# Two transformer blocks in one kernel: the six norm boundaries taken by token tile instead of for both tiles at once

## The chip, the cores and the metric

The kernel runs on one core of one Trainium2 chip. A core has TensorE (PE; PEld is its weight load), VectorE (DVE), ScalarE (ACT), GpSimd (POOL) and SyncE (SP), each with its own instruction stream, which wait for each other through semaphores. The metric is the device time of one execution in microseconds (us), lower is better.

## The reference

One batch of 256 tokens with 1024 features goes through two blocks of one layer each, in float32. Cut to what matters here:

```
def first_block(x, p, positions, ...):
    h = x
    h = h + 0.5 * swiglu(rms_norm(h, ffn1_norm), ffn1_w_in, ffn1_w_out)      # norm n1; hidden width 2816
    u = rms_norm(h, mix_norm)                                                # norm n2
    proj = u @ w_in                     # latents (672 columns), stick-breaking q, k, v, gates
    ... two attentions, merged = g_mla * (o_mla @ w_branch_mla) + g_sb * (o_sb @ w_branch_sb)
    h = h + merged @ w_out
    h = h + 0.5 * swiglu(rms_norm(h, ffn2_norm), ffn2_w_in, ffn2_w_out)      # norm n3
    ple_gate = sigmoid(rms_norm(h, ple_norm) @ w_ple_gate)                   # norm n4
    return h + ple_gate * (p @ w_ple_proj)

def second_block(x, ...):
    proj = rmsnorm(x, attn_norm) @ w_in                                      # norm n5
    ... sparse attention, state-space branch, gates -> merged
    x = x + merged @ w_out
    return x + hier_moe(rmsnorm(x, ffn_norm), router weights, 32 experts)    # norm n6

def rms_norm(x, g):
    r = rsqrt(mean(x * x, axis=-1) + 1e-6)
    return (x * r) * g
def swiglu(u, w_in, w_out):
    a, b = split(u @ w_in, 2)
    return (silu(a) * b) @ w_out
```

## The kernel before, in words

**Data.** X holds the 256 tokens as two tiles of 128 partitions (tokens) by 1024 columns. A norm's output is kept turned: Uh and Ul are 8 chunks of 128 features (partitions) by 256 tokens. Every float32 operand of a matmul is split into a high part and a rest (h and l), and a product is three matmuls (`mm3`): high by high, high by rest, rest by high.

**Weights.** They come in slabs of 1 MB (8 chunks of 128 rows by 256 columns), which SP loads into three slots (NSLOT = 3), each in two halves. ACT copies a half to the high part (L464) once the slab three before it has been used up, and DVE subtracts to get the rest (L470). A semaphore `lo_done` counts halves, `slab_used` counts slabs that PE has finished. `hi_upto(name)` and `lo_upto(name)` issue the splits up to two slabs behind the one named.

**A norm boundary.** X is updated in four parts of 256 columns, both tiles in each. Then ACT takes the sum of squares of each tile (L581), POOL the inverse root (L590, L594), DVE scales a tile into xn (L607), PE transposes the tile's 8 chunks (L621) into banks 4 to 7, both tiles of a chunk side by side, ACT copies with the gain to Uh (L585; for n1 L1340), 8 instructions of 256 columns, and DVE makes Ul (L611), 8 of 256 columns. PE then starts the first matmuls of what follows chunk by chunk as Ul grows. ACT begins with the copies when both tiles are transposed.

**What follows the norms.** After n1 and n3 come the feed-forward loops (`pe_ffn`), 11 rounds of two slabs up (96 matmuls that move 256 token columns) and one slab down (24 that move 512). Four matmuls with zeros (L633) clear the four banks that gather the result. After n2 come the latent slabs `lat0` to `lat2`, after n4 `pproj` (which needs no norm) and four slabs `pgate`, after n5 the slabs `q0`, `q1` and so on, after n6 the router (36 columns), between rows of matmuls with zeros that only keep PE at work (L2509). The slabs `wout` (before n3), `pgate` (before n5) and `wo` (before n6) are matmuls with 128 tokens as weights that move 256 weight columns, tile 0 and then tile 1 in each slab.

**Order.** Every engine's order is the order in which the code is written; nothing reorders it. On ACT, behind the splits of the first three slabs, stand the issue of eleven DMAs of constants (L1343 to L1348, among them the token positions) and two sines of the rotation angles (L1351, L1352), which wait for DVE (L1719) and so for the positions; behind them the first Silu (L675).

Of the kernel before, what the change touches and what calls it, by code (L numbers as in the profile page):

```python
# [15 lines left out]
P = 128  # L16
# [80 lines left out]
def two_blocks(nc, a, out):  # L97
    with ExitStack() as ctx:
        def sb(name, shape, dt=F32, scope=ctx):
# [14 lines left out]
                   (("ss", NT), ("tr", KD // 2), ("hi", KD), ("r", NT), ("xn", NT), ("lo", KD))],  # L114
# [350 lines left out]

        def split_lo(i, q=None):
# [110 lines left out]
        def act_norm(nm, ready, gain):  # L577

            for t in range(NT):
                act.wait_ge(*reach(ready[0], ready[1 + t]))  # L580
                act.activation(xn[:, t], X[:, t], ACT.Square, accum_out=stat("norm", 4)[:, t:t + 1]).then_inc(S(nm + "_ss"), 1)  # L581
            for j in range(KD // 2):
                act.wait_ge(*reach(nm + "_tr", j + 1))
                for c in range(2):
                    act.activation(Uh[:, 2 * j + c], bank[4 + j][:, c * T:(c + 1) * T], ACT.Copy,  # L585
                                   scale=gcol(gain, 2 * j + c)).then_inc(S(nm + "_hi"), 1)
# [17 lines left out]
        def dve_norm(nm, gain):  # L604
            for t in range(NT):
                dve.wait_ge(*reach(nm + "_r", t + 1))
                dve.tensor_scalar(xn[:, t], X[:, t], stat("norm", 4)[:, 2 + t:3 + t], None, ALU.mult).then_inc(S(nm + "_xn"), 1)  # L607
            for j in range(KD // 2):
                dve.wait_ge(*reach(nm + "_hi", 2 * j + 2))
                for c in range(2):  # L610
                    dve.scalar_tensor_tensor(Ul[:, 2 * j + c], bank[4 + j][:, c * T:(c + 1) * T], gcol(gain, 2 * j + c),  # L611
                                             Uh[:, 2 * j + c].bitcast(F32), ALU.mult, ALU.subtract).then_inc(S(nm + "_lo"), 1)

        def pe_norm(nm):
            for t in range(NT):
                pe.wait_ge(*reach(nm + "_xn", t + 1))
                for j in range(KD // 2):
                    if t == 0:
                        claim(4 + j, nm + "_lo", 2 * j + 2)
                    for c in range(2):  # L620
                        last = pe.transpose(bank[4 + j][:, c * T + t * P:c * T + (t + 1) * P],  # L621
                                            xn[:, t, (2 * j + c) * P:(2 * j + c + 1) * P], ident)
                    if t == NT - 1:
                        last.then_inc(S(nm + "_tr"), 1)
            fresh.append((nm + "_lo", 1, Uh))

        def pe_ffn(nm, n):
            b = slab_of[nm]  # L630
# [29 lines left out]
            up(None, b)  # L660
# [564 lines left out]

        gate2_bank = (7, 4, 7, 0, None, None, 6, 7)
# [99 lines left out]
        def _(_e):  # L1326
# [29 lines left out]
            act_norm("n2", ("ffn1_x", 2, 4), "mix_norm")  # L1356
# [1238 lines left out]
```

## Time and profile before

| | us |
|---|---|
| median of 3 runs | 1460.13 (1456.04 to 1461.11) |
| the profiled execution | 1461.1 |
| its span, from the first to the last instruction | 1459.2 |
| PE busy in it | 1359.7 (93%) |
| PE's weight load busy | 1233.4 (85%) |
| DVE busy | 942.3 (65%) |
| ACT busy | 755.8 (52%) |
| mean granted TensorE clock | 0.967 of full |

PE's stream is almost full, so time is lost where PE waits, where its clock is at the lower of its two levels (1.0 of full is 2.4 GHz, 0.5 is 1.2 GHz), and where its instructions get little done each. Durations of matmuls are longer than the distance from one to the next, since they overlap. What a matmul costs in a dense stretch is the length of the stretch divided by the number of matmuls in it; some records are missing and some at the edges are counted, so such a quotient is good to some per cent.

### The profile page before, as it was taken

What the parts mean: (1) busy time and instruction counts of PE and PEld (TensorE: products, weight loads), DVE (VectorE), ACT (ScalarE), POOL (GpSimd) and SP (SyncE); (2) the same over time, 40 slices, a digit from 0 to 9 for tenths busy, and PEclk for the clock granted to TensorE, in tenths of its full rate; (3) what the DMA queues carried; (4) which work ended last, traced back from release to release, by engine and by line L of the source; (5) the groups of instructions that cost most, each with busy time, mean ns of one, the idle gap of its engine ahead of it and who ended that gap; (6) DMA issues with size and microseconds to landing.
All of it is one profiled execution on the core that took longest, in us unless ns stands there. A gap on an engine that the chain in (4) does not pass through costs nothing.

```text
span 1459.2 us, 22962 instructions
## 1 busy us (share of the span) xinstructions
PE 1359.7 (93%) x9038; PEld 1233.4 (85%) x9038; DVE 942.3 (65%) x1363; ACT 755.8 (52%) x1108; POOL 171.6 (12%) x131
## 2 busy tenths in 40 slices
PE   6999999979898999998978997998999999999997
PEld 5999989978698999988977776898999778787776
DVE  4655564473575555565488664575575789999996
ACT  4343344545644343455354556433563577777774
POOL 0211120111001122110020000340000000202020
PEclk9999999989999999999989999999999999999999
DMA  7665645542154655544524222233556299999991
GB/s 243 212 190 178 196 136 162 160 136 96 45 168 141 188 188 184 188 146 143 159 87 144 88 87 87 87 87 93 176 166 205 87 354 366 365 368 351 364 338 60
DMA packets 222164, 263.43 MB, mean 181 GB/s; under 512 B 14017, under 2 KB 204798, under 8 KB 221950
## 3 DMA queue, kind: packets, MB, share of 16 engines
q1 hardware_dynamic: 219520, 260.39, 55.6%
q10 hardware_dynamic: 2558, 1.86, 0.4%
q8 instruction: 58, 0.95, 0.3%
q14 instruction: 28, 0.23, 0.0%
HBM read 261.17 MB, written 1.05 MB: 180 GB/s over the span
## 4 chain that ended last, share of the span: by engine, by line
PE 75%; DVE 14%; ACT 6%; issue 3%; DMA 1%; POOL 1%; ACTq 0%; DVEq 0%; POOLq 0%
PE bank L526 23%; PE bank L528 22%; PE bank L527 22%; DVE sb_wlo L483 3%; DVE sb_wlo L470 3%; ACT sb_whi L464 1%; DVE sb_XC L1870 1%; PE bank L2474 1%; PE bank L621 1%; DMA sb_pos<-in_positions 1%; ACT sb_aw L1542 1%; PE bank L2537 1%; DVE sb_st L1120 1%; DVE sb_aw L1902 1%; ACT sb_sgh L1115 0%
## 5 line engine op out<-in xcount | busy, mean ns | idle before, releaser
L470 DVE TENSOR_TENSOR sb_wlo<-sb_raw,sb_whi 128x1024 fp32r<-128x1024 f32 (+4 forms) x306 | 389.3, 1316 | 239.1 <-ACT sb_whi L464 238.9
L464 ACT ACTIVATE sb_whi<-sb_raw 128x1024 fp32r<-128x1024 f32 (+4 forms) x306 | 301.4, 1037 | 238.6 <-PE bank L528 238.4
L526 PE MATMUL bank<-sb_Uh,sb_whi 128*128 128x256 f32 x1216 | 352.2, 290 | 5.9 <-DVE sb_wlo L470 4.8
L527 PE MATMUL bank<-sb_Ul,sb_whi 128*128 128x256 f32 x1216 | 349.2, 287 | 0.0
L528 PE MATMUL bank<-sb_Uh,sb_wlo 128*128 128x256 f32 x1216 | 348.9, 287 | 0.0
L526 PEld LDWEIGHTS bank<-sb_Uh,sb_whi 128*128 128x128 f32 x1216 | 239.0, 197 | 11.2 <-issue 8.9
L527 PEld LDWEIGHTS bank<-sb_Ul,sb_whi 128*128 128x128 f32 x1216 | 239.1, 197 | 0.8
L528 PEld LDWEIGHTS bank<-sb_Uh,sb_wlo 128*128 128x128 f32 x1216 | 238.6, 196 | 0.0
L526 PE MATMUL bank<-sb_whi,sb_Uh 128*128 128x256 f32 (+3 forms) x560 | 159.8, 285 | 1.1 <-DVE sb_Ul L611 0.7
L527 PE MATMUL bank<-sb_wlo,sb_Uh 128*128 128x256 f32 (+3 forms) x560 | 159.2, 284 | 0.0
L528 PE MATMUL bank<-sb_whi,sb_Ul 128*128 128x256 f32 (+3 forms) x560 | 159.1, 284 | 0.0
L526 PE MATMUL bank<-sb_whi,sb_hh 128*128 128x512 f32 x288 | 113.3, 393 | 3.2 <-DVE sb_hl L907 3.2
L528 PE MATMUL bank<-sb_whi,sb_hl 128*128 128x512 f32 x288 | 112.5, 391 | 0.0
L527 PE MATMUL bank<-sb_wlo,sb_hh 128*128 128x512 f32 x288 | 112.5, 391 | 0.0
L526 PEld LDWEIGHTS bank<-sb_whi,sb_Uh 128*128 128x128 f32 x560 | 108.8, 194 | 2.5 <-issue 1.9
L527 PEld LDWEIGHTS bank<-sb_wlo,sb_Uh 128*128 128x128 f32 x560 | 108.9, 194 | 0.0
L528 PEld LDWEIGHTS bank<-sb_whi,sb_Ul 128*128 128x128 f32 x560 | 108.8, 194 | 0.0
L526 PE MATMUL bank<-sb_whi,sb_SUh 128*128 128x512 f32 x256 | 104.2, 407 | 0.7 <-DVE sb_wlo L483 0.7
L528 PE MATMUL bank<-sb_whi,sb_SUl 128*128 128x512 f32 x256 | 102.0, 398 | 0.0
L527 PE MATMUL bank<-sb_wlo,sb_SUh 128*128 128x512 f32 x256 | 101.7, 397 | 0.0
L483 DVE TENSOR_TENSOR sb_wlo<-sb_raw,sb_whi 128x1024 fp32r<-128x1024 f32 x76 | 90.9, 1220 | 9.3 <-ACT sb_whi L478 9.2
L478 ACT ACTIVATE sb_whi<-sb_raw 128x1024 fp32r<-128x1024 f32 x76 | 78.7, 1057 | 29.5 <-PE bank L528 29.5
(408 smaller groups left out, 2251.8 us busy)
## 6 DMA issues: line engine op xcount, KB each, us to landing
sb_raw<-in_w_in SPq DMA_DIRECT2D x104, 512.0 KB, 4.4
sb_raw<-in_ffn_w_in SPq DMA_DIRECT2D x88, 512.0 KB, 4.6
sb_raw<-in_ffn_w_out SPq DMA_DIRECT2D x44, 512.0 KB, 3.7
sb_raw<-in_w_down SPq DMA_DIRECT2D x26, 512.0 KB, 7.0
sb_raw<-in_w_gate SPq DMA_DIRECT2D x25, 512.0 KB, 6.9
sb_raw<-in_w_up SPq DMA_DIRECT2D x25, 512.0 KB, 6.9
sb_raw<-in_w_out SPq DMA_DIRECT2D x16, 512.0 KB, 4.6
sb_raw<-in_w_ssd_branch SPq DMA_DIRECT2D x16, 512.0 KB, 4.6
```

The source lines that it names most:

```text
L464: nc.scalar.activation(whi[:, i % NSLOT, c], raw[:, i % NSLOT, c], ACT.Copy).then_inc(S("hi_done"), 1)
L470: nc.vector.tensor_tensor(wlo[:, i % NSLOT, c], raw[:, i % NSLOT, c], whi[:, i % NSLOT, c].bitcast(F32), ALU.subtract).then_inc(S("lo_done ...
L478: act.activation(whi[:, i % NSLOT, c], buffers[buffer_of[i]][:, c], ACT.Copy).then_inc(S("hi_done"), 1)
L483: dve.tensor_tensor(wlo[:, i % NSLOT, c], buffers[buffer_of[i]][:, c], whi[:, i % NSLOT, c].bitcast(F32), ALU.subtract).then_inc(S("lo_don ...
L526: pe.matmul(o, lh, rh, start=start, stop=False, skip_group_check=True)
L527: pe.matmul(o, lh, rl, start=False, stop=False, skip_group_check=True)
L528: return pe.matmul(o, ll, rh, start=False, stop=stop, skip_group_check=True)
L621: last = pe.transpose(bank[4 + j][:, c * T + t * P:c * T + (t + 1) * P], xn[:, t, (2 * j + c) * P:(2 * j + c + 1) * P], ident)
L1120: dve.tensor_reduce(stat(nm, 2 * H)[:, t * H:(t + 1) * H], scr[:, 0:H * d].rearrange("p (h d) -> p h d", d=d), AX, ALU.add).then_inc(S(nm ...
L1542: act.activation(aw[:, i % 3, lo:hi], aw[:, i % 3, lo:hi], ACT.Exp, bias=nmx[:, 2 * i + t:2 * i + t + 1], scale=HD ** -0.5, accum_out=sm[: ...
L1870: dve.scalar_tensor_tensor(XC[:, ch, s_:T], sgh[:, j % 2, c * T:(c + 1) * T - s_], gcol("conv_w_2", (TAPS - 1 - s_) * NX + ch), XC[:, ch, ...
L1902: dve.tensor_tensor_reduce(out=aw[:, i % 3, lo:hi], in0=bank[i % 3][:, lo:hi], in1=SELB[:, lo:hi], scale=1.0, scalar=-3e38, op0=ALU.add, o ...
```

## The change

All six norms are taken by token tile. The transposes of a tile go into two banks of their own (even chunks in one, odd chunks in the other; `turn_banks`), ACT and DVE then work on 128 columns at a time, 16 instructions each instead of 8, and ACT's copy of chunk c waits for DVE's work on chunk c - 2, which lies in the same bank.

The output projections before n3, n5 and n6 are taken in pairs of slabs. Each bank then holds one tile by 512 columns. In the second pair both slabs are first used for tile 0 and then for tile 1, so that tile 0 of X is complete a quarter of the projection before its end; its transposes stand inside the last quarter. X is updated by (tile, 512 columns).

What follows a norm starts with tile 0 alone. In the feed-forward parts the first two slabs are taken as tile 0, tile 0, tile 1, tile 1, so each of their matmuls moves 128 columns and there are twice as many; the four zero matmuls stand behind them. `lat0`, `q0` with `q1`, and the router are taken by tile with the same matmuls as before. `pproj` is taken by tile and in halves of 512 columns, one tile ahead of the transposes of n4's tile 0 and one ahead of those of tile 1.

For n1, ACT and DVE split the first two slabs between tile 0 and tile 1 of the norm.

```
-        def pe_norm(nm):
-            for t in range(NT):
-                pe.wait_ge(*reach(nm + "_xn", t + 1))
-                for j in range(KD // 2):
...
-                    for c in range(2):
-                        last = pe.transpose(bank[4 + j][:, c * T + t * P:c * T + (t + 1) * P],
-                                            xn[:, t, (2 * j + c) * P:(2 * j + c + 1) * P], ident)
+        def act_turned(nm, t, gain, chunks=range(KD)):
+            for c in chunks:
+                act.wait_ge(*reach(nm + "_tr", 2 * t + c % 2 + 1))
+                if c >= 2:
+                    act.wait_ge(*reach(nm + "_lo", KD * t + c - 1))
+                act.activation(Uh[:, c, tile_cols(t)], turn_out(nm, t, c), ACT.Copy, scale=gcol(gain, c)).then_inc(S(nm + "_hi"), 1)
+        def dve_turned(nm, t, gain, chunks=range(KD)):
+            for c in chunks:
+                dve.wait_ge(*reach(nm + "_hi", KD * t + c + 1))
+                dve.scalar_tensor_tensor(Ul[:, c, tile_cols(t)], turn_out(nm, t, c), gcol(gain, c),
+                                         Uh[:, c, tile_cols(t)].bitcast(F32), ALU.mult, ALU.subtract).then_inc(S(nm + "_lo"), 1)
+        def pe_turn(nm, t):
+            pe.wait_ge(*reach(nm + "_xn", t + 1))
+            for odd in range(2):
+                claim(turn_banks[nm][2 * t + odd], nm + "_lo", KD * t + KD - 1 + odd)
+                for c in range(odd, KD, 2):
+                    last = pe.transpose(turn_out(nm, t, c), xn[:, t, c * P:(c + 1) * P], ident)
+                last.then_inc(S(nm + "_tr"), 1)
+        def feature_tile(i, b, t, xh, xl, nm=None, at_chunk=None):
+            wh, wl = wslab(i, KD, 256)
+            for k in range(KD):
+                if at_chunk is not None and k == at_chunk[0]:
+                    at_chunk[1]()
+                if k in (0, KD // 2):
+                    pe.wait_ge(*reach("lo_done", 2 * i + (2 if k else 1)))
+                if nm is not None:
+                    pe.wait_ge(*reach(nm + "_lo", KD * t + k + 1))
+                for n in range(2):
+                    f = slice(n * P, (n + 1) * P)
+                    last = mm3(bank[b][:, n * T + t * P:n * T + (t + 1) * P], wh[:, k, f], wl[:, k, f], xh[:, k, tile_cols(t)],
+                               xl[:, k, tile_cols(t)], t + k + n == 0, k == KD - 1)
+            return last
+        def tokens_by_pairs(names, banks, done, made, tile_done, in_last):
...
+                else:
+                    token_tile(s0, b[0], 0, Uh, Ul, KD, 256)
+                    token_tile(s1, b[0], 0, Uh, Ul, KD, 256, at=256, start=False).then_inc(S(tile_done), 1)
+                    token_tile(s0, b[1], 1, Uh, Ul, KD, 256).then_inc(S("slab_used"), 1)
+                    token_tile(s1, b[1], 1, Uh, Ul, KD, 256, at=256, start=False, at_chunk=in_last).then_inc(S("slab_used"), 1)
-        def pe_ffn(nm, n):
+        def pe_ffn(nm, n, norm):
             b = slab_of[nm]
+            feature_tile(b, 4, 0, Uh, Ul, norm)
+            feature_tile(b + 1, 5, 0, Uh, Ul, None, (5, lambda: pe_turn(norm, 1)))
+            feature_tile(b, 4, 1, Uh, Ul, norm).then_inc(S("slab_used"), 1)
+            feature_tile(b + 1, 5, 1, Uh, Ul).then_inc(S("slab_used"), 1)
             for k in range(4):
                 claim(k, nm + "_x", k + 1)
                 pe.matmul(bank[k][:, :], zero[:, 0:P], zero[:, :], start=True, stop=False, skip_group_check=True)
...
-            up(None, b)
             up(1, b + 2)
@@ ScalarE, n1
+            for t in range(NT):
+                act_turned("n1", t, "ffn1_norm")
+                if t == 0:
+                    split_hi(0)
+                    split_hi(1)
+                    nxt["hi"] = 2
@@ VectorE, wout and wo (n3, n6)
+            def add_and_turn(names, tile_done, done, nm, gain):
...
+                add_pair(names, tile_done, 2, done)
+                dve_scaled(nm, 0)
+                nxt["lo"] += 1
+                last = nxt["lo"] - 1
+                half_lo(last, 0)
+                dve_turned(nm, 0, gain, range(0, 4))
+                add_pair(names, tile_done, 3, done)
+                dve_turned(nm, 0, gain, range(4, KD))
+                half_lo(last, 1)
+                dve_scaled(nm, 1)
+                dve_turned(nm, 1, gain)
@@ TensorE, n4 and n5
+            for t in range(NT):
+                for half in range(2):
+                    b = pp_bank[2 * t + half]
+                    claim(b, "pp_ev", 2 * t + half + 1)
+                    last = token_tile(s_, b, t, OMh, OMl, 2, 1024, c0=half * 512, c1=(half + 1) * 512)
+                    last.then_inc(S("pp_mm" if t + half < 2 else "slab_used"), 1)
+                pe_turn("n4", t)
+            tokens_by_pairs([f"pgate{c}" for c in range(4)], pg_bank, "pg", lambda t: ("n4_lo", KD * t, 1), "t_x4",
+                            (6, lambda: pe_turn("n5", 0)))
@@ TensorE, n6
+            token_tile(s_, 0, 0, Uh, Ul, made=("n6_lo", 0, 1), **wide)
+            pe.wait_ge(*reach("x5", 4))
+            idle_turns(8, 1)
+            pe_turn("n6", 1)
             idle_turns(3, 1)
+            token_tile(s_, 0, 1, Uh, Ul, at=256, start=False, made=("n6_lo", KD, 1), **wide).then_inc(S("slab_used"), 1)
```

ScalarE's stream at the start of the program. Before, with `sb_Uh` the gain copies of n1 and `sb_whi` the splits of the first three slabs:

```order
L1335 ACTIVATE sb_xn,sb_st<-sb_X 128x1024 x2
L1340 ACTIVATE sb_Uh<-bank,sb_G 128x256 x8
L464 ACTIVATE sb_whi<-sb_raw 128x1024 x6
L1343 DMA sb_C<-const 128x2292
L1344 DMA sb_pos<-in_positions 128x2x1
```

And now:

```order
L602 ACTIVATE sb_xn,sb_st<-sb_X 128x1024 x2
L609 ACTIVATE sb_Uh<-bank,sb_G 128x128 x8
L465 ACTIVATE sb_whi<-sb_raw 128x1024 x4
L609 ACTIVATE sb_Uh<-bank,sb_G 128x128 x8
L465 ACTIVATE sb_whi<-sb_raw 128x1024 x2
L1424 DMA sb_C<-const 128x2292
L1425 DMA sb_pos<-in_positions 128x2x1
```

Four splits (two slabs) stand ahead of tile 1's copies, and the DMA of the positions stands behind 16 copies instead of 8.

VectorE's stream from `pgate1` to the first slabs behind n5. `sb_sgh<-sb_sgh,sb_GT` is the product with the gate, `sb_X<-sb_X,sb_sgh` the update of X, `sb_xn` the scaling, `sb_Ul` the rest of the norm's output, `sb_wlo` the split of slabs. Before:

```order
L1806 TENSOR_TENSOR sb_sgh<-sb_sgh,sb_GT 128x512
L1809 TENSOR_TENSOR sb_X<-sb_X,sb_sgh 128x2x256
L470 TENSOR_TENSOR sb_wlo<-sb_raw,sb_whi 128x1024 x2
L1806 TENSOR_TENSOR sb_sgh<-sb_sgh,sb_GT 128x512
L1809 TENSOR_TENSOR sb_X<-sb_X,sb_sgh 128x2x256
L607 TENSOR_SCALAR sb_xn<-sb_X,sb_st 128x1024 x2
L611 SCALAR_TENSOR_TENSOR sb_Ul<-bank,sb_G,sb_Uh 128x256 x8
L470 TENSOR_TENSOR sb_wlo<-sb_raw,sb_whi 128x1024 x12
```

And now:

```order
L1945 TENSOR_TENSOR sb_sgh<-sb_sgh,sb_GT 128x512
L1947 TENSOR_TENSOR sb_X<-sb_X,sb_sgh 128x512
L613 TENSOR_SCALAR sb_xn<-sb_X,sb_st 128x1024
L618 SCALAR_TENSOR_TENSOR sb_Ul<-bank,sb_G,sb_Uh 128x128 x4
L1945 TENSOR_TENSOR sb_sgh<-sb_sgh,sb_GT 128x512
L1947 TENSOR_TENSOR sb_X<-sb_X,sb_sgh 128x512
L618 SCALAR_TENSOR_TENSOR sb_Ul<-bank,sb_G,sb_Uh 128x128 x4
L481 TENSOR_TENSOR sb_wlo<-sb_raw,sb_whi 128x1024 x2
L613 TENSOR_SCALAR sb_xn<-sb_X,sb_st 128x1024
L618 SCALAR_TENSOR_TENSOR sb_Ul<-bank,sb_G,sb_Uh 128x128 x8
L481 TENSOR_TENSOR sb_wlo<-sb_raw,sb_whi 128x1024 x12
```

Tile 0 is scaled ahead of the last update of X. Of its 8 chunks four stand ahead of that update and four behind it. The split of slab `q1` has moved behind tile 0's chunks, and tile 1's scaling behind that split.

## Rows read from the trace of the kernel before

**Rows 1.** Page, part 1: busy us, share and instructions by engine.

```profile
PE 1359.7 (93%) x9038; PEld 1233.4 (85%) x9038; DVE 942.3 (65%) x1363; ACT 755.8 (52%) x1108; POOL 171.6 (12%) x131
```

**Rows 2.** Waits of PE: us in total, times, longest.

```profile
PE bank L621 <- DVE sb_xn L607: 14.6, 8, 5.1
```

**Rows 3.** Windows at the boundaries: us, busy (x count) by engine, clock, DMA.

```profile
18.50:33.80 15.30, 14.23 (x96) 14.05 (x96) 6.75 (x17) 3.07 (x7) 0.00 (x0) 0.81 0.80 259
209.10:215.20 6.10, 3.62 (x17) 2.80 (x17) 2.88 (x6) 3.29 (x9) 1.48 (x4) 0.73 0.32 107
439.40:448.10 8.70, 4.67 (x23) 3.58 (x21) 3.96 (x8) 4.83 (x12) 2.00 (x4) 0.80 0.17 54
448.10:459.90 11.80, 11.80 (x98) 11.80 (x99) 3.84 (x7) 6.18 (x9) 0.00 (x0) 1.00 0.29 90
635.00:690.90 55.90, 47.98 (x369) 47.08 (x369) 31.86 (x43) 29.61 (x48) 3.46 (x8) 0.91 0.43 129
669.90:679.10 9.20, 3.86 (x18) 3.30 (x17) 3.52 (x6) 4.28 (x10) 1.98 (x4) 0.65 0.25 84
1136.90:1143.90 7.00, 7.00 (x48) 7.00 (x49) 4.92 (x9) 6.56 (x10) 0.00 (x0) 0.75 0.01 2
1151.40:1158.90 7.50, 7.47 (x32) 6.11 (x33) 6.29 (x14) 4.82 (x7) 0.00 (x0) 1.00 0.39 150
```

**Rows 4.** Windows of dense matmuls (columns as Rows 3): 256 and 160 wide; 256 at half clock.

```profile
451.00:459.00 8.00, 8.00 (x69) 8.00 (x68) 2.25 (x2) 3.29 (x4) 0.00 (x0) 1.00 0.43 133
227.50:231.50 4.00, 4.00 (x38) 4.00 (x38) 2.36 (x2) 2.06 (x3) 0.00 (x0) 1.00 0.46 122
17.40:24.20 6.80, 5.63 (x26) 5.66 (x27) 5.45 (x5) 3.24 (x4) 0.00 (x0) 0.50 0.88 273
```

**Rows 5.** Timeline of PE at full clock: 128-wide rows; start, us, engine, instruction.

```profile
915.32 1.95 PE L2449 MATMUL bank<-sb_C,sb_ssm 128*128 128x128 f32 x16
...
1133.42 1.09 PE L621 MATMUL bank<-sb_C,sb_xn 128*128 128x128 f32 x8 [1.45 <-DVE sb_xn L607]
```

**Rows 6.** Instruction groups by form: busy us, mean ns of one, idle before.

```profile
L585 ACT ACTIVATE sb_Uh<-bank,sb_G 128x256 fp32r<-128x256 f32 x40 | 15.1, 489 | 13.9 <-PE bank L621 13.9
L1542 ACT ACTIVATE sb_aw<-sb_aw,sb_st 128x128 f32<-128x128 f32 x16 | 6.4, 402 | 49.6 <-DVE sb_st L1906 49.6
L611 DVE SCALAR_TENSOR_TENSOR sb_Ul<-bank,sb_G,sb_Uh 128x256 fp32r<-128x256 f32 x48 | 19.4, 477 | 11.0 <-ACT sb_Uh L585 8.3 <-ACT sb_Uh L1340 2.8
L1860 DVE SCALAR_TENSOR_TENSOR sb_aw<-sb_aw,sb_st 128x128 f32<-128x128 f32 x7 | 2.4, 349 | 0.0
```

**Rows 7.** Timeline of the start, all engines (columns as Rows 5).

```profile
9.45 3.67 PE L621 MATMUL bank<-sb_C,sb_xn 128*128 128x128 f32 x16 [1.14 <-DVE sb_xn L607]
...
18.57 0.56 PE L526 MATMUL bank<-sb_Uh,sb_whi 128*128 128x256 f32 x1 [4.08 <-DVE sb_wlo L470]
...
32.87 0.23 ACT L1351 ACTIVATE sb_rope<-sb_rope 128x32 f32<-128x32 f32 x1 [12.23 <-DVE sb_rope L1719]
...
33.85 0.36 PE L526 MATMUL bank<-sb_Uh,sb_whi 128*128 128x256 f32 x1 [1.05 <-ACT sb_sgh L675]
```

**Rows 8.** DMA issues by line: KB, median us to landing.

```profile
sb_pos<-in_positions ACTq DMA_DIRECT2D x1, 1.0 KB, 10.8
```

**Rows 9.** Timeline at n5, all engines.

```profile
672.20 1.06 ACT L581 ACTIVATE sb_xn<-sb_X 128x1024 f32<-128x1024 f32 x1 [1.49 <-DVE sb_X L1809]
...
675.17 3.68 PE L621 MATMUL bank<-sb_C,sb_xn 128*128 128x128 f32 x16 [5.09 <-DVE sb_xn L607]
...
680.65 1.28 ACT L1469 ACT_TABLE_LOAD   x1
```

**Rows 10.** Timeline behind n6, all engines.

```profile
1141.26 2.36 DVE L483 TENSOR_TENSOR sb_wlo<-sb_raw,sb_whi 128x1024 fp32r<-128x1024 f32 x2 [1.80 <-ACT sb_whi L478]
...
1147.04 1.25 PE L2527 MATMUL bank<-sb_aw,sb_C 128*128 128x4 f32 x10
...
1151.42 0.48 PE L2537 MATMUL bank<-sb_PICK,sb_XNh 128*128 128x512 f32 x1 [0.71 <-issue]
```

More of the change, by code:

```diff
@@ new lines, in token_tile @@
+        def token_tile(i, b, t, xh, xl, kc, ncol, at=0, c0=0, c1=None, start=True, made=None, at_chunk=None):
+            wh, wl = wslab(i, kc, ncol)
+            c1 = ncol if c1 is None else c1
+            for k in range(kc):
+                if at_chunk is not None and k == at_chunk[0]:
+                    at_chunk[1]()
+                if k in (0, (kc + 1) // 2):
+                    pe.wait_ge(*reach("lo_done", 2 * i + (2 if k else 1)))
+                if made is not None:
+                    pe.wait_ge(*reach(made[0], made[1] + k // made[2] + 1))
+                last = mm3(bank[b][:, at:at + c1 - c0], xh[:, k, tile_cols(t)], xl[:, k, tile_cols(t)], wh[:, k, c0:c1],
+                           wl[:, k, c0:c1], start and k == 0, k == kc - 1)
+            return last
@@ L1353, in _ @@
             act_ffn("ffn1", NF)
-            act_norm("n2", ("ffn1_x", 2, 4), "mix_norm")
+            for t in range(NT):
+                act_square("n2", t, ("ffn1_x", 2 * t + 2))
+            for t in range(NT):
+                act_turned("n2", t, "mix_norm")
             for i in range(3):
@@ L2322, in _ @@
-            last.then_inc(S("slab_used"), 1)
-            for c in range(4):
-                s_ = need(f"pgate{c}")
-                claim(4 + c, "pg", c + 1)
-                by_token(s_, 4 + c, Uh, Ul, KD, 256).then_inc(S("slab_used"), 1)
-            pe_norm("n5")
+            tokens_by_pairs([f"wout{i}" for i in range(4)], (0, 1, 2, 3), "x2", lambda t: ("mg_lo", 0, 2), "t_x2",
+                            (4, lambda: pe_turn("n3", 0)))
+            pe_ffn("ffn2", NF, "n3")
+            pe.wait_ge(*reach("p_lo", 1))
@@ new lines, in _ @@
+            s_ = slab_of["pproj"]
+            for t in range(NT):
+                for half in range(2):
+                    b = pp_bank[2 * t + half]
[5 more added lines that the diff above has]
+                            (6, lambda: pe_turn("n5", 0)))
@@ new lines, in _ @@
+            for t in range(NT):
+                for i in range(2):
+                    if t == 0:
+                        claim(i, "b2_ev", i + 1)
+                    last = token_tile(slab_of[f"q{i}"], i, t, Uh, Ul, KD, 256, at=256 * t, start=t == 0,
+                                      made=("n5_lo", KD * t, 1) if i == 0 else None,
+                                      at_chunk=(6, lambda: pe_turn("n5", 1)) if (t, i) == (0, 1) else None)
+                    if t:
+                        last.then_inc(S("slab_used"), 1)
```

251 lines of the change are left out of this document (145 added, 106 removed).

## The prediction, made before the changed kernel ran

> **What bounds the kernel now.** I read the page's busy shares first: TensorE is busy 1359.7 of 1459.2 us [rows 1], and no other engine comes near it, so what moves TensorE's stream moves the end. I took every boundary as a stretch of that stream between two points that both kernels have, and asked when PE reaches the second one. Next I read who PE waits for. The largest entry is the transposes waiting for the scaled tile, 14.6 us in 8 waits [rows 2]. That is what the change can take away, apart from what hides behind it. Then I read the windows at the boundaries [rows 3]. The reader is to see two losses in one row: PE is busy for only part of it, and the granted clock is between 1.0 and 0.5, because after the idle time the clock is at its lower level (1.2 GHz) for some microseconds. At n5 it is 9.2 us with PE busy 3.86 and a clock of 0.65.
>
> **What a matmul costs.** Dense matmuls that move 256 columns come every 0.12 us (8.0 us for some 68), those that move 160 every 0.11 us (4.0 us for some 37) [rows 4], and 128 wide 16 take 1.95 us and 8 transposes 1.09 us, with the last one's length inside, so one every 0.11 us [rows 5]. Halving the columns saves 0.009 us of 0.120, since each matmul loads 128 columns of new weights whatever it moves. At half clock one comes every 0.21 to 0.22 us (5.63 us for 26) [rows 4]. I take 0.120 for 256 columns, 0.111 for 128, 0.109 for a transpose and 0.227 for 512 (an estimate: the step from 256 columns to 512 is 256 columns at 2.4 GHz, 0.107 us, on 0.120). The new 128-wide matmuls are between 0.109 (a transpose) and 0.120 (the 256-wide ones).
>
> The Trainium skill (TensorE: Matmul & The Clock Gate, Back-to-back issue gap) has another rule: a stream of weight loads and matmuls would run at about 81 ns per matmul at 128 columns. By it the 384 split matmuls would cost 31.1 us and not 42.6. The rows at 160 and 128 columns, 0.11 us, speak against it for these float32 operands.
>
> **Cost of a norm chunk.** ACT's copy of 256 columns takes 0.489 us and one of 128 columns 0.402; DVE's takes 0.477, and 0.349 at 128 [rows 6]. Now ACT's chunk c waits for DVE's chunk c - 2, so two chunks go round in about 0.39 + 0.35 + 0.04 = 0.78 us, 3.4 us a tile and 6.7 for both. That is more than today's 4.1, so the gain must come from what PE does meanwhile.
>
> **n1, the start: 7.2 us slower.** Today the transposes start at 9.45, the first matmul at 18.57, and the second round's at 33.85, where it had waited for the first Silu [rows 7]. Now tile 0's transposes end by 11.4, its chunks by 14.3, then ACT and DVE split slab 1 (two halves of about 1 us each, DVE's 1.2), so PE starts at 16.35, 2.2 us earlier. From there it has 192 matmuls 128 wide (21.3 us), 8 transposes (0.9) and the four zero matmuls, which today hide in the wait and now stand in the open (0.9). At full clock this ends at 39.4. The granted clock in 17.4 to 24.2 is 0.5 [rows 4], after PE had stood still before 18.57; I expect half of that stretch, which adds 16 x 0.102 = 1.6 us: 41.1 against 33.85. Bounds: 5.5 (no low clock) to 9 (all of it). The Silu is not late: the positions' DMA is issued 3.4 us later, takes 10.8 us to land [rows 8], so the sines come at about 36.5 instead of 32.87 [rows 7], before 41. That is a cover of 4.5 us; without it PE would wait there.
>
> **n2: no change.** In the 6.1 us up to the first latent matmul PE is busy for 3.62 [rows 3]; the idle 2.5 us (squares, root, scaling) stay as they are. Then 8 transposes instead of 16 stand before the first latent matmul, which starts at about 212.9 instead of 215.2; but it is paced by tile 0's chunks, with tile 1's scaling (0.75 us) in the middle of DVE's row, at the low clock, and the other 8 transposes come later. I walk the row to the end of `lat0` and get 221.0 in both. Bounds -1 to +1.5.
>
> **n3: 3.4 us slower.** Today from the last `wout` matmul to the second round: 8.7 + 11.8 = 20.5 us [rows 3]. Now the squares of tile 0 start 5 us before the projection ends and take 3.0 us to the transposes (672.20 to 675.17 is the same chain at n5 [rows 9]), so these find their tile ready inside the last quarter. PE never waits: 16 transposes 1.75, 192 matmuls 21.3, zero matmuls 0.9, together 24.0 us. The bubble of 8.7 us is gone, and 96 matmuls of 11.5 us have become 192 of 21.3. Bounds 2.5 to 5.5. The split of slab 2 and 3 follows `slab_used`, which comes 3 us later; needed 5.8 us after that, it is covered.
>
> **n4 and n5: 8.5 us faster.** From the end of the feed-forward to the start of slab `q2` today: 55.9 us [rows 3]. Nothing here is split into narrower matmuls. The dense sum is `pproj` 24 x 0.227 = 5.4 (48 x 0.12 = 5.8 today), 32 transposes 3.5, `pgate` 192 x 0.12 = 23.0, `q0` and `q1` 11.5: 43.4 us. `pproj` of tile 0 fills n4's wait completely. At n5 something is late next: the last update of X needs sigmoid, product and sum after PE ends the projection (about 2.1 us), and four of tile 0's chunks stand behind it on DVE, so PE waits about 1.5 us in `q0`, 0.7 us for `q1`'s split, which moved behind those chunks, and about 1.1 us at `q2`, since ACT's table load (1.28 us [rows 9]) and `q2`'s split stand behind tile 1's chunks. 43.4 + 3.3 + 0.4 of handovers = 47.1, so -8.8; I take -8.5. Bounds -10 (no bubble at `q1`, `q2`) to -6 (bubbles twice as long).
>
> **n6: 0.8 us slower.** The chain to the experts starts when the router's result and DVE's split before it are done, 14.6 us behind the projection (the split starts at 1141.26 and takes 2.36 [rows 10]). Now the router ends about 4 us earlier, but that split stands behind 16 copies and ends at about 15.0: DVE takes PE's place. Next, the zero matmuls behind the router also end 4 us earlier, and PE then stands still for some 5.8 us up to the small matmuls (now 1147.04). I expect a low clock afterwards, over part of the ten zero matmuls and of the gather that starts at 1151.42: 0.4 us. Bounds -1 to +6.
>
> **Sum.** 7.2 + 0 + 3.4 - 8.5 + 0.8 = +2.9 us on the profiled execution's 1461.1, 1464.0. The median of the runs is 1.0 below that execution, so I predict 1463.
>
> **Rivals.**
> *A, narrow matmuls are cheap.* If the 128-wide matmuls followed the columns (0.107 us per 256 columns, so 0.067), 384 x 0.044 = 17 us would go, but at n1 the Silu stops PE at 37.3 (3.8 us of it) and at n3 tile 1's chunks do (about 6): 1453. The rule of 81 ns would end at the same stops. For it: only the slope above 256 columns. Against: [rows 4, 5].
> *B, the clock behind the router (slower side).* The 5.8 us pause makes the low clock last through the ten zero matmuls and the gather's 32 matmuls (7.5 us at full clock [rows 3]). For it: the router's stretch today has a clock of 0.75 after a smaller pause [rows 3]. Against: the zero matmuls are there to raise the clock again. It decides once the granted clock in the 8 us behind the small matmuls is below about 0.8; in full it costs 6 us more: 1469.
> *C, the change doesn't do what it says.* The round of ACT and DVE (0.39 us a chunk, with waits that the profile of today does not have) is slower than I think, say 0.55, and PE waits at n2 and n5 chunk by chunk: 16 x 0.16 = 2.6 at n2 and as much at n5: 1468.
>
> **Chances.** Forecast 0.62 (1458 to 1467), A 0.08, B 0.15, C 0.12, other 0.03. A measurement of this kernel tells about 0.5% (7.3 us, so 1452.8 and 1467.4) from no change. Faster 0.09 (A and a little of the forecast), slower 0.22 (B, most of C, some of the forecast), within 0.5% 0.69. The range takes in half of B and all of C: 1455 to 1470.
>
> **What would show it.** PE's first matmul at about 16.4 and the second round's at 41; no PE wait at n3 and the first round there 24 us behind the projection; 0.11 us a matmul in the four `feature_tile` blocks with a clock of 1.0; PE waiting about 1.5 us for DVE inside `q0`; `q2` some 47 us behind the feed-forward; the chain behind the router starting as late as today. I am wrong if the feature blocks run at another pace, if PE waits chunk by chunk at n3, or if the clock is low for long in the split blocks.

## The result: 1.3% slower, outside the range

| | us |
|---|---|
| changed kernel, median of 4 runs | 1479.56 (1471.02 to 1486.98) |
| kernel before, median of 4 runs | 1459.48 |
| ratio | 1.0134, 95% interval 1.0105 to 1.0163 |
| profiled execution, and its span | 1486.98, 1485.1 |
| mean granted clock in it, without its start (see below) | 0.976 (before 0.967) |

1463 was predicted, with 1455 to 1470. The change cost 20 us, not 3.

**Profile after.** Part 1 of its page, to be read against [rows 1]:

```profile
PE 1389.3 (94%) x9204; PEld 1261.7 (85%) x9204; DVE 954.4 (64%) x1411; ACT 769.8 (52%) x1156; POOL 172.7 (12%) x131
```

PE has 30 us more busy time for 166 more recorded matmuls. At 0.111 us these would be 18. PE's waits (us in total, times, longest):

```profile
PE bank L2675 <- DVE sb_aw L2199: 4.5, 1, 4.5
...
PE bank L537 <- DVE sb_Ul L1905: 2.3, 1, 2.3
...
PE bank L537 <- DVE sb_Ul L2157: 1.3, 1, 1.3
PE bank L537 <- DVE sb_Ul L618: 1.3, 1, 1.3
PE bank L626 <- DVE sb_xn L613: 1.1, 1, 1.1
```

The transposes' 14.6 us of waiting [rows 2] is down to 1.1. What the change set out to remove is gone, and the time went up all the same. So I read the start, as in [rows 7]:

```profile
9.56 1.97 PE L626 MATMUL bank<-sb_C,sb_xn 128*128 128x128 f32 x8 [1.14 <-DVE sb_xn L613]
...
16.73 0.48 PE L537 MATMUL bank<-sb_Uh,sb_whi 128*128 128x128 f32 x1 [5.20 <-DVE sb_wlo L481]
...
33.43 1.93 PE L626 MATMUL bank<-sb_C,sb_xn 128*128 128x128 f32 x8
...
61.19 0.41 PE L537 MATMUL bank<-sb_Uh,sb_whi 128*128 128x256 f32 x1
```

The first matmul came at 16.73 (16.35 predicted), the second round at 61.19 instead of 33.85 [rows 7]: +27.3 us where +7.2 was forecast. Nothing waits in between. The windows (us, busy by engine, clock, DMA) of n1's two blocks, the dense stretch behind them, and n3's two blocks:

```profile
16.70:33.40 16.70, 16.67 (x78) 16.67 (x79) 3.38 (x3) 1.56 (x2) 0.00 (x0) 1.00 0.46 156
35.50:59.20 23.70, 23.70 (x113) 23.70 (x112) 6.94 (x22) 6.87 (x14) 0.00 (x0) 1.00 0.36 106
61.20:69.00 7.80, 7.80 (x64) 7.80 (x63) 6.24 (x5) 1.92 (x3) 3.54 (x2) 1.00 0.67 202
467.50:476.20 8.70, 8.70 (x80) 8.70 (x80) 3.96 (x8) 2.43 (x7) 1.00 (x2) 1.00 0.34 117
477.20:489.60 12.40, 12.40 (x114) 12.40 (x112) 5.17 (x10) 8.40 (x14) 0.00 (x0) 1.00 0.28 85
```

At n1 a 128-wide matmul took 16.7 / 78 = 0.214 and 23.7 / 113 = 0.210 us, at n3 8.7 / 80 = 0.109: the same instruction in half the time. The clock column misleads in the first two rows. The first clock record of this execution is of full clock, from 62.0 us on, and a window without a record prints 1.00. The distance between the matmuls tells the level, and the experiments below have records of it.

The forms of [rows 6] after: ACT's copy came out at 367 ns (402 taken), DVE's at 349:

```profile
L609 ACT ACTIVATE sb_Uh<-bank,sb_G 128x128 fp32r<-128x128 f32 x96 | 33.5, 367 | 44.0 <-PE bank L626 36.1 <-DVE sb_Ul L618 5.2
...
L618 DVE SCALAR_TENSOR_TENSOR sb_Ul<-bank,sb_G,sb_Uh 128x128 fp32r<-128x128 f32 x96 | 31.9, 349 | 35.3 <-ACT sb_Uh L609 32.0
```

**Stage by stage.** The landmarks are instructions that all kernels have: the first update of X by ffn1 (X1), the copy of the first latents (CQ), the copy to OMh, the first update of X by ffn2 (X2), the last query copy (QT), the last YTh, the first copy of gathered tokens (SUh). The columns are profiled executions, their names those of the experiments:

| from, to | before | after | n1_as_before | n1_warm | pair_by_chunk | n4_n5_alone | all_mended |
|---|---|---|---|---|---|---|---|
| start, X1 (n1) | 207.3 | 234.9 | 207.6 | 215.1 | 209.2 | 207.1 | 207.2 |
| X1, CQ (n2) | 14.0 | 14.6 | 14.7 | 14.0 | 14.0 | 15.8 | 14.0 |
| CQ, OMh (unchanged code) | 198.4 | 195.4 | 198.8 | 195.2 | 195.3 | 195.1 | 194.9 |
| OMh, X2 (n3) | 213.4 | 219.3 | 220.7 | 219.3 | 217.2 | 213.6 | 212.9 |
| X2, QT (n4, n5) | 125.2 | 117.1 | 117.3 | 117.0 | 117.3 | 117.0 | 117.4 |
| QT, YTh (unchanged code) | 304.2 | 304.6 | 307.6 | 307.8 | 306.4 | 304.2 | 304.2 |
| YTh, SUh (n6) | 90.2 | 93.7 | 93.8 | 93.5 | 93.3 | 92.5 | 92.1 |

Stages with unchanged code differ by up to 3.9 us between executions. The granted clock's low stretches differ there: from CQ to OMh the stage took 198.4 us with 17.1 us at the lower level (before) and 195.4 with 10.2 (after), from QT to YTh 304.2 with 34.1 (before) and 307.8 with 51.2 (n1_warm). So a stage can be read to some 2 or 3 us, n1's 27.6 and n4 and n5's 8.1 without doubt.

### The profile page after: what moved, and what is told of

The parts are those of the page before. It is cut to its first block, busy times and chain, and to the rows that moved or that the text cites. A ratio compares the mean times of both kernels' runs of the same rounds, so it can differ in the third digit from the quotient of the medians.

```text
span 1485.1 us, 23489 instructions
## 1 busy us (share of the span) xinstructions
PE 1389.3 (94%) x9204; PEld 1261.7 (85%) x9204; DVE 954.4 (64%) x1411; ACT 769.8 (52%) x1156; POOL 172.7 (12%) x131
## 4 chain that ended last, share of the span: by engine, by line
PE 75%; DVE 15%; ACT 7%; issue 3%; POOL 1%; ACTq 0%; DMA 0%; DVEq 0%; POOLq 0%
PE bank L537 23%; PE bank L539 22%; PE bank L538 22%; DVE sb_wlo L494 3%; DVE sb_wlo L481 3%; DVE sb_XC L2017 1%; PE bank L2623 1%; PE bank L626 1%; ACT sb_whi L465 1%; ACT sb_aw L1646 1%; ACT sb_Uh L609 1%; DVE sb_aw L2049 1%; DVE sb_st L1199 1%; PE bank L2685 0%; ACT sb_XC L1617 0%
## 5 line engine op out<-in xcount | busy, mean ns | idle before, releaser
L481 DVE TENSOR_TENSOR sb_wlo<-sb_raw,sb_whi 128x1024 fp32r<-128x1024 f32 (+2 forms) x304 | 387.0, 1316 | 233.7 <-ACT sb_whi L465 233.5
L537 PE MATMUL bank<-sb_Uh,sb_whi 128*128 128x256 f32 (+1 forms) x1280 | 373.8, 292 | 5.9 <-DVE sb_wlo L481 5.9
L538 PE MATMUL bank<-sb_Ul,sb_whi 128*128 128x256 f32 (+1 forms) x1280 | 371.3, 290 | 0.0
L539 PE MATMUL bank<-sb_Uh,sb_wlo 128*128 128x256 f32 (+1 forms) x1280 | 371.1, 290 | 0.0
L537 PEld LDWEIGHTS bank<-sb_Uh,sb_whi 128*128 128x128 f32 x1280 | 256.0, 200 | 10.4 <-DVE sb_wlo L481 6.5
L538 PEld LDWEIGHTS bank<-sb_Ul,sb_whi 128*128 128x128 f32 x1280 | 256.2, 200 | 0.9
L539 PEld LDWEIGHTS bank<-sb_Uh,sb_wlo 128*128 128x128 f32 x1280 | 255.9, 200 | 0.0
L494 DVE TENSOR_TENSOR sb_wlo<-sb_raw,sb_whi 128x1024 fp32r<-128x1024 f32 x76 | 90.9, 1219 | 9.5 <-ACT sb_whi L489 9.4
```

Of the source, the lines that this page charges most:

```text
L494: dve.tensor_tensor(wlo[:, i % NSLOT, c], buffers[buffer_of[i]][:, c], whi[:, i % NSLOT, c].bitcast(F32), ALU.subtract).then_inc(S("lo_don ...
L537: pe.matmul(o, lh, rh, start=start, stop=False, skip_group_check=True)
L538: pe.matmul(o, lh, rl, start=False, stop=False, skip_group_check=True)
L539: return pe.matmul(o, ll, rh, start=False, stop=stop, skip_group_check=True)
```

## Experiments

The theory was that in n1 the clock was low when the 128-wide matmuls began, and that they don't bring it up. Against it stood the memory traffic at the start, the norm's new order, and chance.

**n1_as_before.** In the changed kernel, n1 and ffn1's first round are the old code, on PE, ACT and DVE. PE's part, cut (`pe_ffn` without a norm takes the zero matmuls first and then a round with 256 columns):

```
-            pe_turn("n1", 0)
-            pe_ffn("ffn1", NF, "n1")
+            pe_norm("n1")
+            pe_ffn("ffn1", NF)
```

> The changed kernel with norm n1 and the first feed-forward round as before (256 columns a matmul, copies of both tiles), all other boundaries by tile. Theory: nearly the whole loss lies at n1, where the 128-wide matmuls came every 0.21 us from 16.7 to 59.2 us. Then the second round starts at 33.9 us again instead of 61.2, and the time is 1479.6 - 27.3 = about 1452 to 1460 (the other boundaries together come to -1.4 us in the two profiles). Rival: the loss is spread over the later boundaries too and the profile of the changed kernel was a poor sample; then it stays above 1465.

1463.53 us, ratio 1.0035 (1.0014 to 1.0056). n1 is back at 207.6 us and 16 us of the 20 are gone: most of the loss lay there. The time was above my 1452 to 1460. The changed stages of the changed kernel's profile other than n1 come to +0.5 +5.9 -8.1 +3.5 = +1.8 us. The measured +5.1 (2.0 to 8.3) lies a little above that; my "-1.4" had counted 4 us that the profile gained in unchanged code. In the table n1 gives back 27.3 us, in the medians 16; after_again below comes back to that.

**width_alone.** In the kernel before, only the matmuls of ffn1's first round are cut in two.

```
+            def narrow(i, b):
...
+                    for t in range(NT):
+                        tk = slice(t * P, (t + 1) * P)
+                        m = mm3(bank[b][:, n * T + t * P:n * T + (t + 1) * P], wh[:, k, f], wl[:, k, f], Uh[:, k, tk], Ul[:, k, tk],
+                                t + k + n == 0, k == KD - 1)
...
+                    elif nm == "ffn1":
+                        narrow(g + j, 4 + j).then_inc(S("slab_used"), 1)
+                        continue
                     by_feature(g + j, 4 + j, Uh, Ul, KD, 256).then_inc(S("slab_used"), 1)
```

> The kernel before with one edit: each matmul of ffn1's first round is cut into two of 128 columns, same order, same norm, same transposes. Theory (width): the clock is low when they start at 18.6 us and they don't bring it up, so 192 matmuls at 0.213 us take 41 us: the second round starts at about 59.5 to 62 us instead of 33.9, and the time is about 1459.5 + 26 = 1485. Rival 1 (the norm by tile, with its splits and transposes between, is what keeps the clock low): the clock rises at about 24 us as before and the round costs 192 x 0.111 = 21.3 us and some low clock: +8 us, about 1467. Rival 2 (each execution draws its own moment at which the clock rises): between the two.

1492.82 us, ratio 1.0211 (1.0166 to 1.0256). Its windows of the round and of what follows:

```profile
18.75:59.40 40.65, 40.65 (x192) 40.65 (x192) 6.68 (x17) 4.91 (x8) 0.00 (x0) 0.50 0.35 114
59.60:69.00 9.40, 9.40 (x66) 9.40 (x66) 8.10 (x6) 3.78 (x4) 4.28 (x2) 0.80 0.56 152
```

And two matmuls of it, the last of the round and the first 256 wide:

```profile
59.34 0.41 PE L528 MATMUL bank<-sb_Uh,sb_wlo 128*128 128x128 f32 x1
59.56 0.52 PE L526 MATMUL bank<-sb_Uh,sb_whi 128*128 128x256 f32 x1
```

Here the clock has records: 0.50, its lower level (1.2 GHz), over 40.65 us in which PE never stood still. Behind it, under 256-wide matmuls, it rises within the window (0.80 is 3.7 us low and 5.7 high). In [rows 4] the 256-wide round started at the same low clock, 0.50, and that was over at 24.2, 5.6 us after its first matmul. In this trace the width alone does it, with the old norm and order, so the new order and waits are not the cause. The median rose by 34 us (24 to 37 by the interval), where 26 were expected. The profiled execution's span is 32.2 us longer: 27.3 of it are at n1 and 4.9 behind it, in code that is the same as before. One of the four executions took 1482.65 us, at a mean clock of 0.958 where the others have 0.948 and 0.949: some 28 us less at the lower level (an estimate: 1480.9 x 0.042 x 2 = 124 us against 1491.4 x 0.051 x 2 = 152). Whether its low stretch at n1 was shorter no trace shows; executions of the kernel before differ as much (0.961 to 0.972).

**n1_warm.** The changed kernel, with matmuls of zeros where PE waits ahead of the narrow ones.

```
+            if norm == "n1":
...
+                for _ in range(24):
+                    pe.matmul(bank[0][:, :], zero[:, 0:P], zero[:, :], start=True, stop=True, skip_group_check=True)
             feature_tile(b, 4, 0, Uh, Ul, norm)
```

> The changed kernel with 24 matmuls of zeros, 512 columns each, between n1's first transposes and the first 128-wide matmul, where PE waits anyway until 16.7 us. Theory (width): they raise the clock, the 128-wide matmuls then keep it and come every 0.11 us; they start at 16.7 to 20 us and the second round at about 41 to 45 us instead of 61.2: about 1462 to 1466. Rival (128-wide matmuls are slow at this place for another reason, such as the full memory traffic at the start, or they let the clock fall again): they still come every 0.21 us, and the time stays near 1480.

1471.43 us, ratio 1.0079 (1.0045 to 1.0113). The windows of the zeros and of the two narrow blocks, and PE's timeline at their two ends:

```profile
11.50:18.20 6.70, 6.70 (x26) 5.49 (x25) 4.92 (x11) 5.61 (x12) 0.00 (x0) 1.00 1.08 352
18.30:26.80 8.50, 8.50 (x78) 8.50 (x77) 2.15 (x2) 0.33 (x1) 0.00 (x0) 1.00 0.76 258
27.80:40.40 12.60, 12.60 (x116) 12.60 (x114) 7.57 (x23) 4.62 (x10) 0.00 (x0) 1.00 0.49 143
```

```profile
11.54 6.89 PE L711 MATMUL bank<-sb_zero 128*128 128x512 f32 x24
18.27 0.22 PE L537 MATMUL bank<-sb_Uh,sb_whi 128*128 128x128 f32 x1
...
41.69 0.35 PE L537 MATMUL bank<-sb_Uh,sb_whi 128*128 128x256 f32 x1
```

This trace's first clock record is of full clock, from 14.1 us on, while the zeros ran. The narrow matmuls now come every 8.5 / 78 = 0.109 us, under more memory traffic (0.76 against 0.46) than when they were slow, and over 22 us of them the clock did not fall. The second round starts at 41.69, +7.8 us, and 23.4 us behind the first matmul, where 21.3 + 0.9 + 0.9 = 23.1 were forecast at full clock. So n1's sum was right but for the clock, and memory traffic is out. The time, 1471.4, is some 5 above what I wrote: the zeros took 19.8 us off n1 in the profiles (234.9 to 215.1), but 8 off the median of the changed kernel. That is the same gap as in n1_as_before.

**n3_behind_a_wait.** n1 as before; at n3 PE is made to wait for both tiles ahead of the narrow round.

```
-    "t_x2", (4, lambda: pe_turn("n3", 0)))
+    "t_x2", None)
+            pe_turn("n3", 0)
+            pe_turn("n3", 1)
             pe_ffn("ffn2", NF, "n3")
```

> n1 as before; at n3 the transposes of both tiles stand ahead of the 128-wide round, so that PE stands still for some 5 us for tile 1's scaling before them. Theory (width): the clock falls in the wait and the 192 matmuls of 128 columns don't raise it: about 41 us instead of 21.3 for them, so it is some 20 to 25 us slower than the kernel with only n1 as before, about 1478. Rival (a low clock lasts only at the start of the program): the clock rises again after 3 to 7 us, and it costs the wait and 1 us: about 6 us slower.

1490.38 us, ratio 1.0207 (1.0173 to 1.0242); 27 us slower than n1_as_before. The windows of the wait and of the low clock behind it:

```profile
438.00:448.00 10.00, 3.74 (x25) 3.50 (x25) 5.67 (x13) 4.27 (x12) 1.00 (x2) 0.79 0.33 105
443.80:491.60 47.80, 45.64 (x210) 45.25 (x211) 9.06 (x15) 10.54 (x18) 3.01 (x3) 0.50 0.11 34
```

PE was busy for 3.74 of 10 us there, with one wait of 6.3 us ahead of tile 1's transposes. Then the clock is at 0.50 for 47.8 us: through the whole narrow round, which begins at 447.58, and until 3 us after the first of the 512-wide zero matmuls (488.58). The loss is above the 20 to 25 us expected. So it isn't the start of the program: n3 got away with its narrow matmuls in the changed kernel only because no wait stood ahead of them.

**pair_by_chunk.** n1 as before, and the first slab of wout and wo is taken chunk by chunk for both tiles.

```
-                    for t in range(NT):
-                        last = token_tile(s0, b[t], t, Uh, Ul, KD, 256, made=made(t))
+                    for k in range(KD):
+                        pe.wait_ge(*reach(made(0)[0], k // made(0)[2] + 1))
+                        for t in range(NT):
+                            last = mm3(bank[b[t]][:, 0:256], Uh[:, k, tile_cols(t)], Ul[:, k, tile_cols(t)], wh[:, k], wl[:, k], ...)
```

> The kernel with n1 as before, and in the first slab of wout and of wo each chunk is taken for both tiles before the next chunk (the tiles still in banks of their own). Theory: in the changed kernel PE came to the last two chunks after 18 matmuls instead of 36 and waited 2.3 us for them at wout and 1.3 us at wo, a wait that the kernel before hid; that wait goes. So from the last copy to OMh to the end of ffn2 it takes 217.1 us instead of 219.3 (before: 213.4), and n6 gets 1.3 us shorter: about 3.4 us faster than the 1463.5 of the kernel with only n1 as before: 1460. Rival: PE gets through wout sooner but then waits for the splits of the next slabs, which hang on the same DVE: no gain.

1459.81 us, ratio 0.9990 (0.9970 to 1.0010): 3.7 us less than n1_as_before by the medians, where 3.4 were expected. The two intervals lie only just apart (1.0010 and 1.0014), so the wait in the trace is the better witness. PE's wait at wout, changed kernel and this one:

```profile
445.71 0.39 PE L537 MATMUL bank<-sb_whi,sb_Uh 128*128 128x256 f32 x1 [2.27 <-DVE sb_Ul L1905]
```

```profile
PE bank L537 <- DVE sb_Ul L1934: 0.4, 1, 0.4
```

OMh to X2 takes 217.2 instead of 219.3. At `wo` the wait of 1.3 us is gone from the waits too, but n6 gets only 0.4 us shorter in the table.

**n4_n5_alone.** The kernel before with n4 and n5 by tile and nothing else (n1, n2, n3 and n6 are the old code).

```
-            pe_norm("n4")
+            for t in range(NT):
+                for half in range(2):
+                    last = token_tile(s_, pp_bank[2 * t + half], t, OMh, OMl, 2, 1024, c0=half * 512, c1=(half + 1) * 512)
+                pe_turn("n4", t)
+            tokens_by_pairs([f"pgate{c}" for c in range(4)], pg_bank, ..., (6, lambda: pe_turn("n5", 0)))
```

> The kernel before with the change at n4 and n5 alone (pproj by tile in the waits, pgate in pairs, q0 and q1 by tile); n1, n2, n3 and n6 as before. Theory: the 8.1 us between the end of ffn2 and the queries, seen in each profile of the changed order, are a gain that stays: 1458.9 - 8 = 1451, range 1449 to 1453. Rival: part of it is only the clock that happened to stay high there, or is given back behind it, and the time comes to 1455 or more.

1452.91 us, ratio 0.9937 (0.9914 to 0.9959): 6.9 us faster than before, and 27 faster than the changed kernel. The window from ffn2's end to `q2`, against 55.9 us at 0.91 [rows 3]; it ends just ahead of `q2`'s start at 681.3, and begins inside ffn2's last matmuls (it ends them at 633.4):

```profile
631.00:681.00 50.00, 47.63 (x356) 45.07 (x354) 35.73 (x61) 33.95 (x64) 4.08 (x8) 1.00 0.42 128
```

681.3 - 633.4 = 47.9 us. The gain is real and stays: every profile with the new order takes 117.0 to 117.5 us from X2 to QT, against 125.2 and 125.4 (before, width_alone). Part of it is the clock: 0.91 over 55.9 us are some 10 us at the lower level, and now there are none in that stretch.

**all_mended.** n1 as before; pairs by chunk; at n3 only the first slab in narrow matmuls; 16 more zeros behind the router.

```
                 feature_tile(b, 4, 0, Uh, Ul, norm)
-                feature_tile(b + 1, 5, 0, Uh, Ul, None, (5, lambda: pe_turn(norm, 1)))
+                pe_turn(norm, 1)
                 feature_tile(b, 4, 1, Uh, Ul, norm).then_inc(S("slab_used"), 1)
-                feature_tile(b + 1, 5, 1, Uh, Ul).then_inc(S("slab_used"), 1)
+                by_feature(b + 1, 5, Uh, Ul, KD, 256).then_inc(S("slab_used"), 1)
...
-            idle_turns(7, 1)
+            idle_turns(23, 1)
```

> n1 as before; wout and wo by chunk in their first slab; at n3 only the first slab of the round is taken by tile and the second with 256 columns (48 + 48 matmuls of 128 columns and 48 of 256, with tile 1's transposes between the tiles); 23 instead of 7 matmuls of zeros behind the router. From rows: n2 +0.5, n3 +5.9 - 2.2 - 4.9 = -1.2 (48 matmuls of 0.12 us for 96 of 0.111), n4 and n5 -8.1, n6 +3.5 - 1.3 - 2.0 = +0.2 (the small matmuls and ten zero matmuls behind the router at full clock). Sum -8.6: about 1450. Rival 1: at n3 PE now waits for tile 1 (its last update of X, squares, root, scaling take 4.9 us, the 48 matmuls that cover it 5.3), the clock falls and the 128-wide matmuls keep it low: 5 to 15 us more. Rival 2: the clock behind the router falls all the same, 2 us more.

1453.65 us, ratio 0.9944 (0.9922 to 0.9967): faster than both kernels, not to be told from n4_n5_alone, and 3.7 us above the 1450 expected. n3 is even with before (212.9 against 213.4), n6 is not. Rival 1 did not come: PE waited 0.5 us for tile 1 and the clock stayed at 1.00. Rival 2 was partly right. The window from the small matmuls behind the router to the gather has a clock of 0.73, in spite of 23 zeros ahead:

```profile
1130.20:1136.50 6.30, 5.51 (x25) 4.22 (x24) 3.98 (x13) 4.49 (x6) 0.00 (x0) 1.00 0.77 251
1136.50:1141.50 5.00, 4.92 (x21) 4.09 (x22) 4.75 (x15) 0.00 (x0) 0.00 (x0) 0.73 0.86 313
```

**after_again.** The changed kernel once more, with no edit.

> The changed kernel itself once more. Theory (the 128-wide matmuls of n1 never raise the clock): again 41 us for them in the profile, the second round at 61 to 62 us, and times of 1471 to 1487, around 1479. Rival (it is drawn anew in each execution when the clock rises in that stretch): in the profile the distance of the matmuls changes to 0.11 us somewhere between 17 and 59 us, and the times spread from about 1463 to 1487.

1479.87 us (1475.18 to 1487.86), ratio 1.0117 (1.0076 to 1.0159). n1's blocks again:

```profile
16.60:33.10 16.50, 16.47 (x77) 16.47 (x78) 3.55 (x3) 2.12 (x2) 0.00 (x0) 1.00 0.49 162
34.90:59.00 24.10, 24.10 (x115) 24.10 (x114) 7.24 (x23) 6.97 (x14) 0.00 (x0) 1.00 0.33 104
```

0.214 and 0.210 us a matmul again. Neither trace shows the clock rising in the narrow blocks, but both belong to the three slowest of this kernel's nine executions, so the rival is not ruled out. The totals even speak for it. Span times mean clock is the span less half of the low clock that is on record. For the kernel before, 23 executions give 1405 to 1413 us. The changed kernel falls into two groups: three executions (spans of 1485.1, 1485.5 and 1486.0 us, clock 0.976) give 1449 to 1450, and the other six (1469.2 to 1478.1 us, 0.971 to 0.979) give 1435 to 1438. The two profiled executions are in the first group and have no clock record for their first 62 us. If the six also have a record only from the first rise on, that rise came some 2 x 13.9 = 28 us earlier, at about 34 us, where tile 0's narrow block ends. This is an estimate from totals, and no trace shows it. It would save 14 us at n1, and so explain why the median rose by 20 us and not by the profiles' 26, and why n1_as_before and n1_warm won back less than the table's n1. What decides between the two groups stays open.

## Why the prediction was wrong

**n1, the step that failed: "I expect half of that stretch, which adds 16 x 0.102 = 1.6 us".** I had taken the length of the low clock from the old kernel (17.4 to 24.2) as if it were a matter of time. It depends on what runs in it. Under 256-wide matmuls it was over at 24.2; under 128-wide ones it lasted as long as they did, in four traces of three kernels, 41 to 48 us. In the profiled execution all 192 matmuls at 0.213 instead of 0.111 us are 19.6 us where 1.6 were counted, 18.0 too few. The eight transposes and four zeros among and behind them are some 1.6 more (8 x 0.1 and 4 x 0.2), and the first matmul came 0.4 later (16.73, 16.35 forecast). That is the 20 us between 7.2 and the measured 27.3. By the medians the error is smaller: n1 cost 16.0 us (changed kernel against n1_as_before) where 7.2 were forecast, 8.8 us more, which the estimate under after_again would explain. My bound of 9 came from the same error. The rest of the step held: 41.69 for the second round at full clock in n1_warm (41.1). The Silu was not late, but the cover forecast for it was hardly there: the sines came at 47.95 us in the changed kernel and at 40.71 in n1_warm (where PE had begun 1.9 us later than forecast), not at 36.5. In n1_warm that is 1.0 us ahead of the second round, not 4.5, and the Silu ended 0.1 us ahead of it.

**The width.** 0.109 us at full clock, 0.111 taken; rival A is out. The price per matmul that the prediction took from [rows 4, 5] held at full clock. The Trainium skill's rule of about 81 ns at 128 columns (TensorE: Matmul & The Clock Gate, Back-to-back issue gap) would have made the 80 of n3's window 6.5 us; the trace has 8.7.

**n3, +3.4 forecast, +5.9 measured.** From the end of the projection the step held. The zeros stand at 490.07 and the second round at 490.76:

```profile
490.07 0.85 PE L716 MATMUL bank<-sb_zero 128*128 128x512 f32 x3
490.76 0.28 PE L537 MATMUL bank<-sb_Uh,sb_whi 128*128 128x256 f32 x1
```

That is 23.3 us behind the last `wout` matmul (467.5), and 0.9 of transposes lie ahead of it: 24.2, where 24.0 was forecast. Missed was the other end of the projection: by tile, PE reaches the last two chunks of the merged rows after 18 matmuls instead of 36 and waits 2.3 us. I had priced the wait removed and not looked at what feeds the first slab. pair_by_chunk took it away.

**n4 and n5, -8.5 forecast, -8.1 measured**, by the steps foreseen: 47.9 us (47.1), a wait in `q0` for tile 0's chunks behind the last update of X, one for `q1`'s split, 0.9 us at `q2`, and the clock at 1.0 throughout:

```profile
700.58 0.35 PE L537 MATMUL bank<-sb_whi,sb_Uh 128*128 128x256 f32 x1 [1.28 <-DVE sb_Ul L618]
...
702.82 0.36 PE L537 MATMUL bank<-sb_whi,sb_Uh 128*128 128x256 f32 x1 [0.51 <-DVE sb_wlo L481]
```

Forecast were 1.5, 0.7 and 1.1. n4 gave 4.6 of it (from the end of ffn2 to the first `pgate` matmul 7.3 us instead of 11.9), n5 3.4.

**n2, 0 forecast**, 14.6 against 14.0 us. The new order took 14.0 to 14.8 us in seven traces and the old one 14.0 to 15.8 in three: right within what can be read.

**n6, +0.8 forecast, +3.5 measured, part of it perhaps chance.** The pause behind the router is there (4.5 us of 5.8 forecast), and rival B's low clock too:

```profile
1172.00 2.29 PE L2675 MATMUL bank<-sb_aw,sb_C 128*128 128x4 f32 x10 [4.51 <-DVE sb_aw L2199]
1174.15 4.39 PE L2655 MATMUL bank<-sb_zero 128*128 128x512 f32 x10
...
1178.38 0.39 PE L2685 MATMUL bank<-sb_PICK,sb_XNh 128*128 128x512 f32 x1
```

```profile
1165.80:1172.00 6.20, 1.69 (x8) 1.04 (x7) 4.02 (x14) 4.30 (x5) 0.00 (x0) 0.95 0.77 257
1172.00:1178.40 6.40, 6.40 (x21) 5.49 (x22) 5.14 (x16) 0.00 (x0) 0.00 (x0) 0.52 0.67 242
```

Small matmuls to gather took 6.4 us instead of 4.4 (1147.04 to 1151.42, [rows 10]), so the clock cost 2.0. B's sign, a clock below 0.8 in these 8 us, is met (0.62 from 1172.0 to 1180.0), but by 1178.4, when the gather begins, it was up again, which is why B's 6 us did not come. With the wait of 1.3 us for the last chunk at `wo` that makes 3.3. But the old code took 90.2, 90.9 (width_alone) and 92.5 us in this stage, so between 1 us and all of the +3.5 is the change's. This stays open.

**The sum.** 27.6 + 0.5 + 5.9 - 8.1 + 3.5 = +29.4, and -4 in unchanged code, for the profiled executions; by medians it was +20, for the reason given under after_again if its estimate holds. The boundaries other than n1 came to +1.8 where -4.3 was forecast (+4.7 by the median of n1_as_before), mostly since n3 and n6 cost 5.2 us more. So by medians n1's clock is about half of the miss, and the rest of the boundaries the other half; in the profiles it is 20 us against 6.

## What to carry to other kernels

A low clock isn't a fixed price: ask what runs while it is low, and put wide matmuls there; narrow ones belong where PE is already at full clock and nothing waits ahead of them. Here, of six boundaries, the two where existing work filled the wait gained 8 us, and the two that cut matmuls narrower to fill it lost: take such a change boundary by boundary. And when the profiled execution is among the slowest of its kernel, hold its stages against the medians before you trust their size. When a projection is reordered so that its end comes early, look at what its first matmuls wait for as well.

## What the runs showed of the hardware

- A stream of 128-wide float32 matmuls with a new weight load each, PE without a pause, left the clock at 1.2 GHz for 40.65 us (width_alone, 0.50 in the window) and for 47.8 us with the wait ahead of it and the start of wide matmuls behind it (n3_behind_a_wait). The same stream left it at 2.4 GHz for 22 us once it was there (n1_warm). Whether a stream that begins low stays low in every execution is not shown: the totals of six executions of the changed kernel suggest a rise at about 34 us (an estimate, see after_again).
- At the low clock the width made no difference to the distance: 0.212 us (40.65 / 192) at 128 columns, 0.217 (5.63 / 26) at 256 [rows 4]. At the high one it was 0.109 and 0.12.
- The same code took up to 3.9 us more or less in two executions (194.9 to 198.8 from CQ to OMh), with 10.2 to 13.7 us at the lower clock in those of 194.9 to 195.4 and 17.1 to 20.5 in those of 198.4 and 198.8.
